# Layer 0's second norm for the latent tokens between the context's output products, the context's sums of squares by token, and TensorE's order behind them by readiness

## The reference, cut to what matters

```python
x = x + g1 * m
h = modulate(x, norm_ffn_g[l], sh2, sc2)
x = x + g2 * hierarchical_moe(h, ...)
```

## Time and profile before

| | |
|---|---|
| runs | 761.48, 763.27 (median), 763.44 us |
| profiled execution | 759.59 us, its span 757.5 us |
| busy in the span | PE 85%, DVE 39%, ACT 18%, POOL 16% |
| granted TensorE clock, mean | 0.939 |
| HBM | 284.68 MB read, 17.56 MB written, 399 GB/s over the span |

### The profile page before, as it was taken

The page is one execution under the profiler, slowest core; times in us unless marked ns, Lnnn a source line. Parts: engine busy times, 40 slices in busy tenths (PEclk is TensorE's granted clock), DMA queues, the critical chain, the costliest instruction groups (busy, mean ns, idle before and its releaser), DMA issues.

```text
span 757.5 us, 12788 instructions
## 1 busy us (share of the span) xinstructions
PE 647.5 (85%) x4711; PEld 349.6 (46%) x4711; DVE 297.0 (39%) x724; ACT 133.1 (18%) x330; POOL 120.6 (16%) x194
## 2 busy tenths in 40 slices
PE   4999999999999999999745678899999997564586
PEld 3533343436795755554322333647655553222242
DVE  2114618674315544444311113666544443112123
ACT  5002234553127200000000000654000000000000
POOL 1000000001000133333211001010343333111110
PEclk9999999999999999999966689999999999677799
DMA  9999959959089699999999999999999999999997
GB/s 330 422 430 427 415 235 391 399 220 418 31 333 387 263 395 424 416 420 416 422 424 420 424 420 376 416 427 418 374 419 408 421 422 417 420 422 422 423 419 291
DMA packets 40009, 291.12 MB, mean 384 GB/s; under 512 B 7514, under 2 KB 8946, under 8 KB 20496
## 3 DMA queue, kind: packets, MB, share of 16 engines
q1 hardware_dynamic: 30544, 272.46, 87.0%
q0 software_dynamic: 7600, 12.81, 4.8%
q10 hardware_dynamic: 1808, 5.06, 1.7%
HBM read 284.68 MB, written 17.56 MB: 399 GB/s over the span
## 4 chain that ended last, share of the span: by engine, by line
PE 63%; DMA 25%; DVE 4%; SPq 4%; issue 2%; ACT 1%; DVEq 0%; POOLq 0%; POOL 0%
PE bank L1804 17%; DMA ring<-in_moe_w_in 9%; PE bank L1490 8%; PE bank L1841 8%; PE bank L1400 5%; DMA cond_at<-in_moe_w_in 4%; DMA ring<-in_moe_w_out 4%; PE bank L1604 4%; DMA adas<-in_moe_w_in 3%; PE bank L1763 2%; PE bank L1612 2%; DMA adaw<-rows,gidx 2%; PE bank L1543 2%; PE bank L1564 2%; PE bank L1708 2%
## 5 line engine op out<-in xcount | busy, mean ns | idle before, releaser
L1804 PE MATMUL bank<-ring,qkv 128*32 128x256 f32 (+1 forms) x1344 | 135.5, 428 | 38.5 <-DMA ring<-in_moe_w_in 25.8
L1804 PEld LDWEIGHTS bank<-ring,qkv 128*32 128x32 f32 (+1 forms) x1344 | 77.4, 134 | 82.3 <-issue 52.5
L1232 DVE COPY qkv<-bank 128x512 f32<-128x512 f32 x44 | 30.4, 692 | 200.7 <-PE bank L1763 200.7
L607 POOL DMA_INDIRECT results<-adaw,scur x46 | 47.2, 1027 | 249.8 <-DVE adaw L1255 218.0
L883 ACT ACTIVATE qkv<-bank 128x128 f32<-128x128 f32 x48 | 13.3, 278 | 408.4 <-PE bank L1804 408.4
L1841 PE MATMUL bank<-ring,qkv 128*32 128x512 f32 (+1 forms) x368 | 65.7, 601 | 1.4 <-DMA ring<-in_moe_w_out 1.4
L1490 PE MATMUL bank<-ring,hT 128*128 128x512 f32 x144 | 64.6, 599 | 1.8 <-DVE hT L973 1.8
L1804 PE MATMUL bank<-seventh,qkv 128*64 128x256 f32 (+1 forms) x224 | 35.4, 483 | 16.7 <-DMA ring<-in_moe_w_in 16.7
L597 POOL DMA_INDIRECT adaw<-rows,gcur x40 | 41.6, 1040 | 33.0 <-POOL gcur L594 27.7
L1490 PEld LDWEIGHTS bank<-ring,hT 128*128 128x128 f32 x144 | 26.5, 190 | 37.9 <-issue 35.2
L1804 PE MATMUL bank<-xT,qkv 128*64 128x256 f32 (+1 forms) x192 | 30.8, 486 | 14.4 <-DMA cond_at<-in_moe_w_in 14.4
(11 more groups left out here) (266 smaller groups left out, 837.0 us busy)
## 6 DMA issues: line engine op xcount, KB each, us to landing
ring<-in_moe_w_in SPq DMA_DIRECT2D x37, 2048.0 KB, 17.1
ring<-in_moe_w_out SPq DMA_DIRECT2D x44, 1024.0 KB, 26.7
ring<-in_ada_w SPq DMA_DIRECT2D x14, 2048.0 KB, 13.6
adaw<-in_ada_w SPq DMA_DIRECT2D x10, 2048.0 KB, 14.9
adaw<-in_moe_w_in SPq DMA_DIRECT2D x8, 2048.0 KB, 22.3
seventh<-in_moe_w_in SPq DMA_DIRECT2D x8, 1792.0 KB, 25.0
xT<-in_moe_w_in SPq DMA_DIRECT2D x8, 1536.0 KB, 20.2
hT<-in_moe_w_out SPq DMA_DIRECT2D x10, 1024.0 KB, 25.2
```

The source lines that it names most:

```text
L607: pool.indirect_dma_start(res, bass.IndirectOffsetOnAxis(ap=scur[:, p, :], axis=0), yout[:, p], None, bounds_check=res_limit, oob_is_err=F ...
L1232: V.tensor_copy(xgT[:, p], bank[2][:, :]).then_inc(xgT_ready, 1)
L1804: last = T.matmul(bank[p][64 * a + m * h:64 * a + m * (h + 1), 0:2 * P], xk[:, k % 4, k // 4, m * h:m * (h + 1)], gate_up_of(b, k)[:, :, a ...
```

## The change

It splits the second norm of layer 0 by kind of token. ACT squares the latents' columns in the steps of the attention loop, one step behind their sum. The latents' sums, their turning and spreading, and `vectors(3)` stand between the context's output products on PE; DVE's factors, its scaling and the vectors' sums stand between the context's sums into `xT`, and ACT modulates the latents in the same stretch. The context's squares are added up by token: the squares are the weights and one column of ones moves, so that the sum comes out by token and needs no copy and no turning. Behind the products PE takes what is ready: the latents' logits, the spreading of the context's factor, the context's logits, with half of the context's blocks modulated by ACT. All six `keep` move behind the logits, two of them ahead of the turning of the logits and four behind it, the latents' tiles first. The norm of layer 1 stays as it was.

```diff
...
-sums = free[:, 3200:3200 + NTOK]
+sums = free[:, 3584:3584 + NTOK]
+sq_context = free[:, 0:KD * CTX].rearrange("p (k n) -> p k n", k=KD)
+sq_latent = free[:, QKV:QKV + KD * (NTOK - CTX)].rearrange("p (k n) -> p k n", k=KD)
...
-KEEP_BANKS = (1, 5, 3, 0, 1, 3)
+CONTEXT_BANK = 5
+KEPT = ((2, 3, 4, 5, 0, 1), (0, 1, 2, 3, 4, 5))
+KEEP_BANKS = ((0, 3, 1, 2, 0, 3), (1, 5, 3, 0, 1, 3))
...
-        sp.wait_ge(xr_ready, l * KD + KD)
+        sp.wait_ge(xr_ready, 2 * KD + l * KD)
...
+    def latent_square(k):
+        act.wait_ge(x_new[0], k + 1)
+        A.activation(sq_latent[:, k], xT[:, k, CTX:NTOK], ACT.Square).then_inc(sq_ready, 1)
...
+        if u - 1 in WO_STEPS:
+            latent_square(WO_STEPS[u - 1])
...
+    def latent_norm_act(i):
+        if i == 0:
+            act.wait_ge(st_mm, 1)
+            A.activation(sums[:, CTX:NTOK], bank[STAT_BANKS[0]][:, CTX:NTOK], ACT.Copy).then_inc(std_ready, 1)
+        else:
+            act.wait_ge(st_mm, 2)
+            A.activation(ss[:, 9:11], bank[STAT_BANKS[0]][:, NTOK + 1:NTOK + TT], ACT.Sqrt, scale=1.0 / (32 * D),
+                         bias=C("eps")).then_inc(std_ready, 1)
...
+    def latent_modulate(k):
+        act.wait_ge(xr_ready, k + 1)
+        A.activation(hT[:, k, CTX:NTOK], hT[:, k, CTX:NTOK], ACT.Identity, bias=mod(0, 3, k, 1),
...
+    def context_square(k):
+        act.wait_ge(x_new[0], KD + k + 1)
+        A.activation(sq_context[:, k], xT[:, k, 0:CTX], ACT.Square).then_inc(sq_ready, 1)
...
+    def first_norm_act():
+        act.wait_ge(s_out, 32)
+        context_square(0)
+        latent_norm_act(0)
+        latent_norm_act(1)
+        for k in range(1, 3):
+            context_square(k)
+        for k in range(KD):
+            latent_modulate(k)
+            if k % 2:
+                context_square(3 + k // 2)
+        context_square(KD - 1)
+        act.wait_ge(st_mm, 4)
+        A.activation(ss[:, 8:9], bank[CONTEXT_BANK][:, CTX:CTX + 1], ACT.Sqrt, scale=1.0 / D, bias=C("eps"))\
+            .then_inc(std_ready, 1)
+        for k in range(1, KD, 2):
+            act.wait_ge(xr_ready, KD + k + 1)
+            A.activation(hT[:, k, 0:CTX], hT[:, k, 0:CTX], ACT.Identity, bias=mod(0, 3, k, 0),
+                         scale=mod(0, 4, k, 0)).then_inc(h_new, 1)
...
+        if l == 0:
+            first_norm_act()
...
         act.wait_ge(lgT_mm, l + 1)
         A.activation(rt[0:NG + NE, 160:160 + NTOK], bank[7][0:NG + NE, 0:NTOK], ACT.Copy).then_inc(lgT_copied, 1)
-        keep(4)
-        keep(5)
+        for n in range(0 if l == 0 else 4, 6):
+            keep(n)
...
+    def latent_factors():
+        dve.wait_ge(std_ready, 2)
+        order(V.reciprocal(ss[:, 13:15], ss[:, 9:11]))
+        V.tensor_tensor(dg[:, 1:TT, :], ident.unsqueeze(1).to_broadcast([P, TT - 1, P]),
+                        ss[:, 13:15].unsqueeze(2).to_broadcast([P, TT - 1, P]), ALU.mult).then_inc(root_ready, 1)
...
+    def latent_scaled(k):
+        dve.wait_ge(st_mm, 3)
+        V.tensor_tensor(hT[:, k, CTX:NTOK], xT[:, k, CTX:NTOK], bank[STAT_BANKS[0]][:, CTX:NTOK], ALU.mult)\
+            .then_inc(xr_ready, 1)
...
     for d in range(KD):
         dve.wait_ge(mix_mm[0], KD + d + 1)
         V.scalar_tensor_tensor(xT[:, d, 0:CTX], bank[3 + d % 2][:, 0:CTX], mod(0, 2, d, 0),
                                xT[:, d, 0:CTX], ALU.mult, ALU.add).then_inc(x_new[0], 1)
+        if d == 0:
+            dve.wait_ge(ada_vec, 4)
+            modulation(3, 0, 5, 6)
+            vectors_of(3, 1, 0, 6 * KD)
+            V.memset(ss[:, 17:18], 0.0).then_inc(mods_ready, 1)
+        elif d == 1:
+            latent_factors()
+        if 2 <= d < 6:
+            latent_scaled(2 * d - 4)
+            latent_scaled(2 * d - 3)
...
+    def first_norm_dve():
+        stat = bank[CONTEXT_BANK]
+        dve.wait_ge(std_ready, 3)
+        order(V.reciprocal(ss[:, 12:13], ss[:, 8:9]))
+        V.tensor_scalar(dg[:, 0], ident, ss[:, 12:13], None, ALU.mult).then_inc(root_ready, 1)
+        dve.wait_ge(st_mm, 5)
+        for k in range(0, KD, 2):
+            for j in range(2):
+                V.tensor_tensor(hT[:, k + j, 0:CTX], xT[:, k + j, 0:CTX], stat[:, 2 * CTX:3 * CTX], ALU.mult)\
+                    .then_inc(xr_ready, 1)
+            dve.wait_ge(xr_ready, KD + k + 1)
+            V.tensor_scalar(hT[:, k, 0:CTX], hT[:, k, 0:CTX], mod(0, 4, k, 0), mod(0, 3, k, 0),
+                            ALU.mult, ALU.add).then_inc(h_ctx, 1)
...
-    norm_dve(0, 0, 4, 3, lambda k: hT[:, k, 0:CTX])
-    dve.wait_ge(ada_vec, 4)
-    modulation(3, 0, 5, 6)
-    vectors_of(3, 1, 0, 6 * KD)
-    V.memset(ss[:, 17:18], 0.0).then_inc(mods_ready, 1)
+    first_norm_dve()
...
+    def latent_sums():
+        stat = bank[STAT_BANKS[0]]
+        for k in range(KD):
+            pe.wait_ge(sq_ready, k + 1)
+            j = 32 * (k % 4)
+            last = T.matmul(stat[j:j + 32, CTX:NTOK], ones[:, 0:32], sq_latent[:, k], start=k < 4, stop=k >= 4,
+                            skip_group_check=True)
+        last.then_inc(st_mm, 1)
...
+    def latent_turned_sums():
+        pe.wait_ge(std_ready, 1)
+        for t in range(1, TT):
+            last = T.matmul(bank[STAT_BANKS[0]][:, NTOK + t:NTOK + t + 1], sums[:, t * P:(t + 1) * P], ones[:, 0:1],
+                            start=True, stop=True)
+        last.then_inc(st_mm, 1)
...
+    def latent_spread():
+        pe.wait_ge(root_ready, 1)
+        T.matmul(bank[STAT_BANKS[0]][:, CTX:NTOK], ones, dg[:, 1:TT, :].rearrange("p t n -> p (t n)"),
+                 start=True, stop=True).then_inc(st_mm, 1)
...
+    def context_sum(k):
+        pe.wait_ge(sq_ready, KD + k + 1)
+        return T.matmul(bank[CONTEXT_BANK][:, CTX:CTX + 1], sq_context[:, k], ones[:, 0:1], start=k == 0, stop=k == KD - 1,
+                        skip_group_check=True)
...
     for d in range(KD):
...
         last.then_inc(mix_mm[0], 1)
+        if d == 0:
+            latent_sums()
+            vectors(3)
+        elif d == 1:
+            latent_turned_sums()
+        elif d == 2:
+            latent_spread()
+        elif d == 3:
+            pe.wait_ge(s_wr, 16)
+        elif d >= 5:
+            for k in range(2 * d - 10, 2 * d - 8):
+                context_sum(k)
...
-        t, q = n // 2, n % 2
-        if n == 4:
+        t, q = KEPT[l][n] // 2, KEPT[l][n] % 2
+        if l == 0 and n > 3:
+            pe.wait_ge(x1_copied, n - 3)
...
-            last = T.transpose(bank[KEEP_BANKS[n]][:, k * P:(k + 1) * P], xT[:, 4 * q + k, t * P:(t + 1) * P], ident)
+            last = T.transpose(bank[KEEP_BANKS[l][n]][:, k * P:(k + 1) * P], xT[:, 4 * q + k, t * P:(t + 1) * P], ident)
...
+    def logits(l, k, a, b):
+        return T.matmul(bank[7][0:NG + NE, a:b], wr[:, l, k, :], hT[:, k, a:b], start=k == 0, stop=k == KD - 1,
+                        skip_group_check=True)
...
+    def latent_logits(blocks):
+        for k in blocks:
+            pe.wait_ge(h_new, k + 1)
+            logits(0, k, CTX, NTOK)
...
+    def first_norm_pe():
+        context_sum(KD - 2)
+        latent_logits(range(1))
+        context_sum(KD - 1).then_inc(st_mm, 1)
+        latent_logits(range(1, 4))
+        pe.wait_ge(root_ready, 2)
+        T.matmul(bank[CONTEXT_BANK][:, 2 * CTX:3 * CTX], ones, dg[:, 0], start=True, stop=True).then_inc(st_mm, 1)
+        latent_logits(range(4, KD))
         for k in range(KD):
...
+            if k % 2:
+                pe.wait_ge(h_new, KD + k // 2 + 1)
+            else:
+                pe.wait_ge(h_ctx, k // 2 + 1)
+            last = logits(0, k, 0, CTX)
+        last.then_inc(lgT_mm, 1)
+        keep(0, 0)
+        keep(0, 1)
...
-            pe.wait_ge(x_new[0], KD)
-            vectors(3)
-        keep(l, 4)
-        keep(l, 5)
-        if l == 0:
-            pe.wait_ge(s_wr, 16)
-        for k in range(KD):
-            pe.wait_ge(h_new, l * KD + k + 1)
-            pe.wait_ge(h_ctx, l * KD + k + 1)
-            last = T.matmul(bank[7][0:NG + NE, 0:NTOK], wr[:, l, k, :], hT[:, k, :], start=k == 0, stop=k == KD - 1)
-        last.then_inc(lgT_mm, 1)
+            first_norm_pe()
...
+        if l == 0:
+            for n in range(2, 6):
+                keep(0, n)
         for n in range(6):
+            if l == 0 and n == 2:
+                pe.wait_ge(x1_copied, 5)
             rows_by_token(n)
...
+        if l == 0:
+            pe.wait_ge(x1_copied, 6)
...
```

More of the change, by code:

```diff
@@ new lines, in second_norm_act @@
+            def second_norm_act():
+                for i in range(KD):
+                    act.wait_ge(x_new[2], 2 * (i + 1))
+                    A.activation(sq[:, i], xT[:, POOL_ORDER[i], :], ACT.Square).then_inc(sq_ready, 1)
+                act.wait_ge(st_mm, 6)
+                A.activation(sums, bank[STAT_BANKS[1]][:, 0:NTOK], ACT.Copy).then_inc(std_ready, 1)
+                act.wait_ge(st_mm, 7)
+                A.activation(ss[:, 8:11], bank[STAT_BANKS[1]][:, NTOK:NTOK + TT], ACT.Sqrt, scale=1.0 / (32 * D), bias=C("eps"))\
@@ L844, in keep @@
```

(49 more changed lines are left out.)

53 lines of the change are left out of this document (21 added, 32 removed).

## The result

| | before | after |
|---|---|---|
| median of the runs | 762.55 us (761.48 to 763.78, 10 runs) | 768.50 us (762.03 to 771.58, 10 runs) |
| ratio | | 1.0067, 95% interval 1.0044 to 1.0090 |
| profiled execution, its span | 759.59, 757.5 us | 768.87, 767.0 us |
| granted TensorE clock, mean | 0.939 | 0.933 |

The changed kernel is slower by 0.4 to 0.9%. I had forecast no change, 763.4, and a range up to 765.8; the median lies beyond it. The runs before lie within 2.3 us of each other, the runs after within 9.6: whatever costs the time does not cost the same in each execution.

What follows compares the result with a forecast made beforehand. The prediction took the stream of expert weights, with two gated gaps, to bound the kernel. Logits 2.0 us earlier and counts 2.2 later gave +0.2 us, about 763.4 us from a median of 763.27; range 761.3 to 765.8.

Steps and rivals of the forecast that it cites:

- the sum: Logits 2.0 us earlier, counts 2.2 later behind them: +0.2 us at tile 0, the second gate and the end.
- the second gate: Expert load in SP's queue issued at 258.06, when tile 0 has left its place; forecast to move +0.2 us.
- part 4: Work moved behind the logits, six `keep` included: counts come 2.2 us later after the logits, released by PE.
- what none of them names: Remainder for causes outside forecast and rivals: chance 0.06, split 0.03 faster and 0.03 slower.
- Part 1: Work put between PE's products ahead of the last one: 4.2 us, so products end near 231.0.
- Part 2: Weight stream: first gap grows to 6.3 us, second shrinks from 5.6 to almost nothing; gain at most 1.4 us.
- first gap: Stretch from 225.4 to 227.5 where the weight stream stands nearly still, ended by expert 2's load; forecast 6.3 us.
- Part 3: Logits behind the products on PE: they end near 237.7, 2.0 us earlier.
- The floor: Rival: tile 0 ends 1.6 us earlier, but the weight stream limits the gain to 1.4; 761.9 us, chance 0.13.
- the gather: Rival: the gather for tile 2 takes 8.4 us against 6.88, +1.5 on the chain; 764.9 us, chance 0.13.
- The clock: Rival: TensorE's clock falls during the transposes behind the logits, +1.5 to +3.0 us to tile 0; 765.7 us, chance 0.10.

Runs made afterwards that it cites:

- one trace without `busy`: Changed kernel without `busy(7, 2)` in layer 0 and with 96 idle instructions over eight tiles of layer 0; 763.99 us, ratio 1.0022.
- the run with 64: Changed kernel with 64 idle PE instructions, 8 ahead of each of eight tiles of layer 0; 762.28 us, ratio 1.0000.
- 96 with and without `busy`: Changed kernel with 96 idle instructions, 12 per tile: 762.70 us, ratio 0.9999; the same without `busy(7, 2)` in layer 0: 763.99 us, ratio 1.0022.
- 120: Kernel before with 120 idle PE instructions, 15 ahead of each of eight tiles of layer 0; 763.09 us, ratio 1.0008.
- the two runs with 200: Changed kernel with 200 idle PE instructions, in one place of layer 0: 774.39 us, ratio 1.017; spread over eight tiles: 770.93 us, ratio 1.0098.

## Why the prediction was wrong

**The step that failed** is the last of the sum: "+0.2 us at tile 0, hence at the second gate and at the end". The figure at tile 0 missed by 1.1 us (-0.9 measured, part 4 below), which is less than the 2.3 that the forecast counts as noise; what failed is the word "hence". It took everything behind tile 0 to be as before, because its work is the same. But PE's program is one line of code, and 56 instructions more at one place move all that lies behind. In place of nothing, the runs showed 4.3 to 4.5 us of PE standing at a branch at the end of layer 1, and sums behind it that took 1.7 us longer at a lower clock: 6.0 in all, at a place where the work is the same. None of the rivals named that; it fell into the 0.06 for "what none of them names". With the stall kept away, the changed kernel's ratio is 1.0000 and 0.9999, with intervals of 0.2% and less to each side: the forecast of no change, for the change itself, held. In part that is luck: it was forecast from +0.2 at tile 0, and it came with -0.9 there and waits at the layers' ends that no one forecast (below).

Point by point, the 1.65 taken off where a time is given:

- **Part 1**, 4.2 us of PE's work ahead of the last product: expert 2's load is issued 21.80 us behind the first batch in place of 17.93, so 3.9. The row's price of the one-column products was the right one for products that each load their own weights, and not the 25 ns of the Trainium skill's page TensorE: Matmul & The Clock Gate (Back-to-back issue gap): four took 0.50, in the timeline of PE:

```profile
215.85 1.07 PE L1700 MATMUL bank<-qkv,con 128*32 128x256 f32 x16
...
219.63 0.50 PE L1707 MATMUL bank<-con,qkv 128*128 128x1 f32 x4
...
221.86 0.60 PE L1713 MATMUL bank<-dg,con 128*128 128x256 f32 x2
```

- **Part 2**, a first gap of 6.3 us and hardly a second: 6.1, and some 2 at a share of 0.70. Right.
- **Part 3**, logits done near 237.7: 237.5. The multiplication of 128 columns, bounded between 0.26 and 0.55, took 0.28 in DVE's line:

```profile
L1162 DVE TENSOR_TENSOR hT<-xT,bank x8: 277/280/289, 235.6 to 237.8; 128x128 f32<-128x128 f32 x8
```

- **Part 4**, counts 2.2 us later behind the logits: they begin at 244.74, released by PE itself, 7.24 behind the logits' end in place of 5.78, so 1.5 later. The sum at tile 0 was then about -0.9, not +0.2, and the gather, 7.44 in place of 6.88, took 0.6 of it back: that is the direction that the rival of the gather named, less than half of its 1.5, and harmless.
- **The floor** wasn't tested: no run made tile 0 early enough to reach it.
- **The clock**, the rival on the slow side, did not come true: 1.00 from the products to tile 0. That the clock can fall there is shown by one trace without `busy`; the price there was 3.2 us from the first batch of loads, a little over the rival's 1.5 to 3.0.

**What stays open.** At the end of layer 0 PE's wait for the last weights was 0.68 us before and 2.35 after:

```profile
469.87 1.92 PE L1841 MATMUL bank<-ring,qkv 128*32 128x512 f32 x16 [0.68 <-DMA ring<-in_moe_w_out]
```

```profile
472.61 2.78 PE L2000 MATMUL bank<-ring,qkv 128*32 128x512 f32 x16 [2.35 <-DMA ring<-in_moe_w_out]
```

The products behind it run at a lower clock, as at the end. The kernel before shows the same wait with 56 idle instructions (2.24) and not with 28 (0.68), so it isn't the norm. But here the code arrives in time, and the wait is on a transfer whose last bytes come late. Which of the transfers holds them up, I couldn't tell from traces that don't tell the 16 DMA engines apart. It doesn't decide the time: the run with 64 has such waits at the ends of both layers, and no loss in its median. At the end of layer 1 the wait follows the place of the code: 2.1 to 2.3 us in the four traces whose packet came early (64, 96 with and without `busy`, 120), 0.6 to 0.8 in the other eight. So even the good places here may cost something. Of the changed kernel with `busy`, only the two runs with 200 have neither the stall nor this wait, and they pay for their idle instructions.

## What to carry to other kernels

Count the instructions that a change adds to each engine's queue, also where the work is hidden: they move everything behind them, and a jump over code that doesn't run can come to land where the next 16 KB haven't arrived. A stall called "issue", behind a branch, on an engine whose work didn't change, is the sign of it; the branch's own duration in the trace (5.67 us in place of 0.22) is the proof. The test is cheap: put as many idle instructions into the kernel before, and a few more into the changed one. And before a change is dropped as slower, it should be measured with its code in another place.

## What the runs showed that I had not expected

- A fetch of 16 KB of PE's code can come too late: its packet started 6.0 to 7.0 us behind the first load of 3 MB of results, and PE stood for 4.3 to 4.5 us, in three profiles out of three with that alignment.
- The stall costs more than its length: the granted clock was 0.72 behind it, and 6.6 us of sums took 8.3.
- A wait on a semaphore that is long satisfied is not free on PE: some 0.05 us each, 0.10 to 0.11 us per instruction of two (21.53 us for 200).
